# RWKV inverse: streaming only the 32 changed columns of each 64-column block

## The chip, the cores and the metric

The kernel runs on one core of one Trainium2 chip. The metric is device time in microseconds (us) from the start to the end of one execution; the median of three runs stands for it. Engines are named as in the profile: PE is TensorE (matmul), PEld is TensorE's weight load, DVE VectorE, ACT ScalarE, POOL GpSimd, SP SyncE, which only issues transfers.

## The reference

A two-layer backbone on 512 latent and 256 context tokens, width 1024, all in fp32. Layer 0 is grouped-query attention with an MLP, layer 1 a bidirectional RWKV-7 time mixing with an MLP. The part that matters here is the RWKV scan, per direction and head, with a 64x64 state S:

```
sa = S a_t
S  = S * w_t + sa b_t^T + v_t k_t^T
y  = S r_t
```

The kernel computes it in 12 chunks of 64 tokens. Inside a chunk the terms `sa` depend on each other through a unit triangular 64x64 matrix L, and the kernel needs the inverse of I + L (with the sign folded in) for each chunk and head. The reference has no such inverse; it is a consequence of the chunked form.

## The kernel before

Work before and after the RWKV core (attention, projections, MLPs) is big matmuls, mostly at L398. The core itself (`slots`, L1210) has 16 passes q = 2g + d: eight groups g of two heads, each in two directions d. Pass q is done in three parts that overlap with the parts of other passes: `pre` (decays, keys, the triangular matrices into MT) in slot q, `inverse` in slot q + 1, `chain` (the recurrence over the 12 chunks) in slot q + 2. The strings SLOT (L1205) write the order out by hand: every engine goes through the same list of letters p, i and c, and each letter lets one of its three generators issue its next piece. So TensorE, which is in order, meets the pieces of the inverse between those of the recurrence. Waits on semaphores inside the pieces keep the data in order.

The inverse works by doubling. Level l (0 to 5) joins blocks of width w = 2^l to blocks of 2w. XI is the inverse so far, XIT its transpose. 24 matrices (12 chunks x 2 heads) are kept as three groups of four units u, each unit holding two matrices, one in each half of the 128 partitions (HALVES). Step n = 3l + i handles group i at level l:

- the *update* U = MT^T XI into PSUM bank 0 (L1495, 8 matmuls of 64x64 by 64x64). For n < 3, at level 0, the moving operand is the identity (IDN) and not XI.
- VectorE multiplies it with the level's mask (L1547). The mask holds the identity plus the entries that this level joins, which all lie in one half of the columns: those whose block number is odd for d = 0 (even for d = 1). The product is UM (for n < 3 it is XI itself). UM shares memory with AR and shows as AR in the trace.
- the *level products* for v = n from 3 on, one step later in the order: `product_xi` (L1470) forms the next XI into bank 1, `product_xit` (L1480) the next XIT into bank 2; at the last level, v >= 15, only `product_xit` is made, into both banks.
- ScalarE copies out of banks 1 and 2 only the half of the columns that the level changes (`every_other`, L1517, L1528 and L1531), and at the last level everything, into XIF (L1535).

Before the change every matmul of these three lines streams all 64 columns of its moving operand, whatever the level. The stationary operand (the weights) always has 64 columns. In the trace's names "PS<-XI,MT" the moving operand stands first and the weights second.

Two other lines serve as comparison: L2151 (128 weight columns, 2 streamed columns, in the first 60 us) and L1254 (the cumulated decays of a pass, 128 weight columns, 128 streamed columns).

Of the kernel before, what the change touches and what calls it, by code (L numbers as in the profile page):

```python
# [34 lines left out]
C = 64  # L35
# [88 lines left out]
def build(nc, a, out):  # L124

    stack = ExitStack()
    with stack:
# [28 lines left out]
        IDN, HEAD1, SWAP, SEL = CK[:, 0:128], CK[:, 128:256], CK[:, 256:384], CK[:, 384:386]  # L156
# [55 lines left out]
        def core(name, shape, dt=F32):  # L212

            t = place(name, core_at[0], shape, dt)
            core_at[0] += -(-math.prod(shape[1:]) // 64) / 4
            return t
# [19 lines left out]
        XI = core("XI", [P, 12, C])  # L236
        XIT = core("XIT", [P, 12, C])
# [9 lines left out]
        UM = [AR[b][:, 0:4, 1, :] for b in (1, 2)]  # L247
# [10 lines left out]
        def bank(b):  # L258
            return PS[:, b * 512:(b + 1) * 512]
# [929 lines left out]
        def mt_at(u):  # L1189
            m, h = divmod(u, 2)  # L1190
            return 256 * m + 128 * h if m < TC // P else 512 * (m - 1) + 256 * h

        def mt(b, u, part):


            return MT[b][:, mt_at(u) + part * C:mt_at(u) + part * C + C]
# [268 lines left out]
        def pe_inverse(e, q):  # L1465
            d, b = q % 2, q % 3

            def product_xi(v, i, cp):
                t, o = HALVES[cp], HALVES[1 - cp]
                return e.matmul(bank(1)[t, i * C:(i + 1) * C], XIT[o, 4 * (v % 3) + i, :], UM[v % 2][o, i, :], start=True,  # L1470
                                stop=True, skip_group_check=True)

            def product_xit(v, i, cp):

                o = HALVES[1 - cp]
                if v < 15:
                    out = bank(2)[o, i * C:(i + 1) * C]
                else:
                    out = bank(1 + i % 2)[HALVES[cp ^ (i % 2)], i // 2 * C:(i // 2 + 1) * C]
                return e.matmul(out, UM[v % 2][o, i, :], XIT[o, 4 * (v % 3) + i, :], start=True, stop=True,  # L1480
                                skip_group_check=True)

            for n in range(19):
                if n < 18:
                    e.wait_ge(um_ready, 18 * q + n)
                    if n < 3:
                        e.wait_ge(lta_ready, 3 * q + n + 1)
                    elif n >= 6:
                        e.wait_ge(xi_ready, 12 * q + n - 5)
                    e.nop(nofuse=True)  # L1490
                    for i in range(4):
                        for cp, t in enumerate(HALVES):
                            u = 4 * (n % 3) + i
                            o = HALVES[1 - cp] if n >= 3 else t
                            mm = e.matmul(bank(0)[o, i * C:(i + 1) * C], mt(b, u, 0)[t],  # L1495
                                          XI[t, u, :] if n >= 3 else IDN[t, t], start=True, stop=True,
                                          skip_group_check=True)
                    mm.then_inc(u_done, 1)
                yield
                if n >= 4:  # L1500
                    v = n - 1
                    e.wait_ge(um_ready, 18 * q + v + 1)
                    if v < 6:
                        e.wait_ge(xit_init, 6 * q + 2 * (v % 3) + 2)
                    e.wait_ge(xit_ready, 15 * q + v - 3)
                    if v < 15:
                        e.wait_ge(xi_ready, 12 * q + v - 3)
                    e.nop(nofuse=True)
                    for i in range(4):
                        for cp in range(2):  # L1510
                            if v < 15:
                                product_xi(v, i, cp)
                            mm = product_xit(v, i, cp)
                    mm.then_inc(inv_done, 1)
                yield
# [605 lines left out]
        def _(pe):  # L2121
# [117 lines left out]
            pe.wait_ge(evac_dve, U_OUT1 + 2)  # L2239
            pe.wait_ge(pads_ready, PADS)  # L2240
            slots(pe, pe_pre, pe_inverse, pe_chain)

            def og_split(e, k):
# [224 lines left out]
```

## Time and profile before

| what | value |
|---|---|
| median of 3 runs | 2493.08 us (2490.87 to 2499.34) |
| profiled execution, its own time | 2491.33 us |
| its span (first to last instruction) | 2489.1 us |
| PE busy | 2303.2 us (93%) |
| DVE, ACT, POOL busy | 1096.6, 916.0, 660.8 us |
| mean granted TensorE clock | 0.984 |

A page of the profile gives busy times of each engine, the span in 40 slices, the chain of work that ended last and the costliest groups of instructions. Rows of groups read "line engine operation out<-in shape xcount". A matmul shape "64*64 64x64" is 64 rows by 64 columns of weights, and a moving operand of 64 partitions by 64 columns. The granted clock is 1.00 at TensorE's full 2.4 GHz and 0.50 at 1.2 GHz; a stretch's number is the mean. Matmuls of one burst overlap, so their durations don't add; what counts is the distance from start to start.

### The profile page before, as it was taken

How to read it: one execution, taken by the hardware profiler on the slowest of the kernel's cores; microseconds unless marked ns; L12 is line 12 of the kernel's file. 1: busy time of each engine (PE TensorE's matmuls, PEld its weight loads, DVE VectorE, ACT ScalarE, POOL GpSimd, SP SyncE). 2: the span in 40 equal slices, each digit the busy share in tenths (PEclk: the TensorE clock that was granted, in tenths of full speed). 3: DMA queues.
4: the chain of work that ended last, by engine and by line, in shares of the span. 5: the costliest groups of instructions: out<-in, count | busy, mean ns of one | idle time of the engine just before them, and what ended most of it. 6: DMA issues, size and time to landing. Idle time of an engine off the chain costs nothing.

```text
span 2489.1 us, 65277 instructions
## 1 busy us (share of the span) xinstructions
PE 2303.2 (93%) x27611; PEld 1905.8 (77%) x27611; DVE 1096.6 (44%) x2418; ACT 916.0 (37%) x1627; POOL 660.8 (27%) x481
## 2 busy tenths in 40 slices
PE   5998899899999999999988888888888889999998
PEld 3776677788888888878857777777777768888887
DVE  2326666451121211463355666666666645411213
ACT  3555555352120312452224344244244223422324
POOL 0334555303322332213301111111121110344442
PEclk9999999999999999999999999999999999999999
DMA  8124556112122112123410000000000011323321
GB/s 250 52 51 153 172 171 184 39 63 69 51 68 67 54 64 68 51 77 119 136 50 23 12 15 23 12 15 23 12 15 23 4 53 52 102 85 101 101 94 59
DMA packets 172316, 176.38 MB, mean 71 GB/s; under 512 B 26512, under 2 KB 160032, under 8 KB 172064
## 3 DMA queue, kind: packets, MB, share of 16 engines
q1 hardware_dynamic: 172064, 172.62, 22.2%
q8 instruction: 207, 3.39, 0.6%
q14 instruction: 45, 0.37, 0.1%
HBM read 161.06 MB, written 11.53 MB: 69 GB/s over the span
## 4 chain that ended last, share of the span: by engine, by line
PE 83%; DVE 7%; issue 5%; ACT 4%; POOL 1%; SPq 0%; DMA 0%; ACTq 0%; DVEq 0%; PEldq 0%
PE PS L398 38%; PE PS L1495 5%; PE PS L576 4%; PE PS L418 3%; PE PS L1480 2%; PE PS L773 2%; PE PS L754 2%; PE PS L1634 2%; PE PS L1307 2%; PE PS L1470 2%; PE PS L733 2%; PE PS L1579 1%; PE PS L763 1%; PE PS L1140 1%; PE PS L1240 1%
## 5 line engine op out<-in xcount | busy, mean ns | idle before, releaser
L378 POOL TENSOR_TENSOR WL<-RAW,WH 128x1024 fp32r<-128x1024 f32 x160 | 383.5, 2418 | 953.0 <-ACT WH L359 953.0
L398 PE MATMUL PS<-AH,WH 128*128 128x256 f32 (+1 forms) x992 | 350.9, 354 | 3.3 <-DVE AL L2356 2.4
L398 PE MATMUL PS<-AH,WL 128*128 128x256 f32 (+1 forms) x992 | 351.6, 354 | 0.0
L398 PE MATMUL PS<-AL,WH 128*128 128x256 f32 (+1 forms) x992 | 349.1, 352 | 0.0
L359 ACT ACTIVATE WH<-RAW 128x1024 fp32r<-128x1024 f32 x160 | 160.1, 1049 | 272.1 <-PE PS L398 265.6
L398 PE MATMUL PS<-BH,WL 128*128 128x512 f32 (+1 forms) x672 | 239.2, 356 | 0.0
L398 PE MATMUL PS<-BH,WH 128*128 128x512 f32 (+1 forms) x672 | 238.5, 355 | 0.0
L398 PE MATMUL PS<-BL,WH 128*128 128x512 f32 (+1 forms) x672 | 237.6, 354 | 0.0
L398 PEld LDWEIGHTS PS<-AH,WH 128*128 128x128 f32 x992 | 187.7, 189 | 31.6 <-issue 2.6
L398 PEld LDWEIGHTS PS<-AL,WH 128*128 128x128 f32 x992 | 186.9, 188 | 27.2
L398 PEld LDWEIGHTS PS<-AH,WL 128*128 128x128 f32 x992 | 187.6, 189 | 25.1
L696 DVE SCALAR_TENSOR_TENSOR X<-PS,MOD,X 128x256 f32 (+3 forms) x92 | 54.8, 652 | 341.8 <-PE PS L398 341.8
L672 DVE TENSOR_TENSOR HSQ<-HRL 128x768 f32<-128x768 f32 (+1 forms) x64 | 51.8, 851 | 317.5 <-ACT HRL L660 317.5
L1480 PE MATMUL PS<-XIT,AR 64*64 64x64 f32 x3840 | 163.3, 226 | 21.9 <-issue 21.8
L1495 PE MATMUL PS<-XI,MT 64*64 64x64 f32 x3840 | 166.9, 223 | 6.3 <-issue 3.8
L1457 POOL TENSOR_TENSOR MT<-MT,CT 128x256 f32<-128x256 f32 x48 | 39.3, 818 | 501.2 <-DVE MT L1439 501.2
L875 POOL TENSOR_TENSOR PB<-PB,SMS 128x768 f32<-128x768 f32 (+1 forms) x96 | 123.9, 1301 | 123.1 <-DVE SMS L897 122.7
L1480 PEld LDWEIGHTS PS<-XIT,AR 64*64 64x64 f32 x3840 | 128.9, 134 | 34.9 <-issue 33.6
L1495 PEld LDWEIGHTS PS<-XI,MT 64*64 64x64 f32 x3840 | 138.7, 136 | 21.1 <-issue 16.0
L1470 PE MATMUL PS<-AR,XIT 64*64 64x64 f32 x3072 | 137.6, 223 | 15.6 <-issue 12.0
L1528 ACT ACTIVATE XI<-PS 128x128 f32<-128x128 f32 x192 | 53.6, 279 | 255.9 <-PE PS L1480 255.5
L660 ACT ACTIVATE HRL<-PS 128x768 f32<-128x768 f32 (+1 forms) x64 | 41.7, 705 | 273.6 <-PE PS L398 262.3
(278 smaller groups left out, 5019.5 us busy)
## 6 DMA issues: line engine op xcount, KB each, us to landing
ADW<-l_ada_w SPq DMA_DIRECT2D x40, 1024.0 KB, 5.4
RAW<-l_mlp_up SPq DMA_DIRECT2D x64, 512.0 KB, 4.5
RAW<-l_mlp_down SPq DMA_DIRECT2D x64, 512.0 KB, 4.3
RAW<-l_w_rkv SPq DMA_DIRECT2D x24, 512.0 KB, 5.0
rwkv_scratch<-STG SPq DMA_DIRECT2D x24, 384.0 KB, 3.2
ADA<-l_ada_w SPq DMA_DIRECT2D x4, 2048.0 KB, 15.6
RAW<-l_w_in SPq DMA_DIRECT2D x16, 256.0 KB, 5.5
RAW<-l_w_out SPq DMA_DIRECT2D x16, 256.0 KB, 5.2
```

The lines of the kernel that those rows point to most:

```text
L359: e.activation(WH[:, s, rows], RAW[:, s, rows], ACT.Copy).then_inc(w_high[h], 1)
L378: e.tensor_tensor(WL[:, s, rows], RAW[:, s, rows], WH[:, s, rows], ALU.subtract).then_inc(w_split[h], 1)
L398: mm = e.matmul(dst, w[:, s, k, n * P:(n + 1) * P], r[:, k, lo:hi], start=(k == 0 and i == 0), stop=(k == KT - 1 and i == 2), skip_group_c ...
L418: mm = e.matmul(dst, w[:, s, k, n * P:(n + 1) * P], r[:, k, lo:hi], start=(k == 0 and i == 0), stop=(k == KT - 1 and i == 2), skip_group_c ...
L576: mm = e.matmul(tile_ps(4 * s + 2 * n)[:, at:at + hi - lo], w[:, s, k, n * P:(n + 1) * P], r[:, k, lo:hi], start=(k == 0 and x == 0), stop ...
L672: e.tensor_tensor(HSQ[:, n, lo:], HRL[:, n, lo:], HRL[:, n, lo:], ALU.mult).then_inc(h_sq, 1)
L696: ins = e.scalar_tensor_tensor(out=x, in0=tile_ps(4 * s + 2 * n)[:, a0:a1], scalar=gate, in1=x, op0=ALU.mult, op1=ALU.add)
L875: e.tensor_tensor(p, p, SMS[:, rs:rs + 1].to_broadcast([P, span(m) * P]), ALU.mult).then_inc(p_scaled, 1)
L1470: return e.matmul(bank(1)[t, i * C:(i + 1) * C], XIT[o, 4 * (v % 3) + i, :], UM[v % 2][o, i, :], start=True, stop=True, skip_group_check=True)
L1480: return e.matmul(out, UM[v % 2][o, i, :], XIT[o, 4 * (v % 3) + i, :], start=True, stop=True, skip_group_check=True)
L1495: mm = e.matmul(bank(0)[o, i * C:(i + 1) * C], mt(b, u, 0)[t], XI[t, u, :] if n >= 3 else IDN[t, t], start=True, stop=True, skip_group_che ...
L1528: e.activation(every_other(XI[:, four, :], v // 3, q % 2), every_other(bank(1)[:, 0:256].rearrange("p (u t) -> p u t", u=4), v // 3, q % 2 ...
```

## The change

`columns(ap, level, odd)` takes from the last 64 columns the blocks of width 2^level whose number is odd (or even), 32 columns in all. The update at L1495 for n >= 3, `product_xi`, and `product_xit` for v < 15 now stream only these columns of the moving operand and write only the same columns in PSUM. The last level's `product_xit` and the first three updates keep 64 columns, as do all weights, all masks, all copies and all waits.

```diff
@@ pe_inverse
+            def columns(ap, level, odd):
+                return ap.rearrange("p (b two w) -> p b two w", two=2, w=1 << level)[:, :, odd, :]
+
             def product_xi(v, i, cp):
                 t, o = HALVES[cp], HALVES[1 - cp]
-                return e.matmul(bank(1)[t, i * C:(i + 1) * C], XIT[o, 4 * (v % 3) + i, :], UM[v % 2][o, i, :], start=True,
-                                stop=True, skip_group_check=True)
+                return e.matmul(columns(bank(1)[t, i * C:(i + 1) * C], v // 3, d), XIT[o, 4 * (v % 3) + i, :],
+                                columns(UM[v % 2][o, i, :], v // 3, d), start=True, stop=True, skip_group_check=True)
 
             def product_xit(v, i, cp):
 
                 o = HALVES[1 - cp]
+                rows = XIT[o, 4 * (v % 3) + i, :]
                 if v < 15:
-                    out = bank(2)[o, i * C:(i + 1) * C]
+                    out = columns(bank(2)[o, i * C:(i + 1) * C], v // 3, 1 - d)
+                    rows = columns(rows, v // 3, 1 - d)
                 else:
                     out = bank(1 + i % 2)[HALVES[cp ^ (i % 2)], i // 2 * C:(i // 2 + 1) * C]
-                return e.matmul(out, UM[v % 2][o, i, :], XIT[o, 4 * (v % 3) + i, :], start=True, stop=True,
-                                skip_group_check=True)
+                return e.matmul(out, UM[v % 2][o, i, :], rows, start=True, stop=True, skip_group_check=True)
 
@@ the update
-                            mm = e.matmul(bank(0)[o, i * C:(i + 1) * C], mt(b, u, 0)[t],
-                                          XI[t, u, :] if n >= 3 else IDN[t, t], start=True, stop=True,
-                                          skip_group_check=True)
+                            out, rows = bank(0)[o, i * C:(i + 1) * C], IDN[t, t]
+                            if n >= 3:
+                                out, rows = columns(out, n // 3, d), columns(XI[t, u, :], n // 3, d)
+                            mm = e.matmul(out, mt(b, u, 0)[t], rows, start=True, stop=True, skip_group_check=True)
```

## Rows read from the trace of the kernel before

**Rows 1.** The page: busy time, then the chain's shares by engine and by line
```profile
PE 2303.2 (93%) x27611; PEld 1905.8 (77%) x27611; DVE 1096.6 (44%) x2418; ACT 916.0 (37%) x1627; POOL 660.8 (27%) x481
...
PE 83%; DVE 7%; issue 5%; ACT 4%; POOL 1%; SPq 0%; DMA 0%; ACTq 0%; DVEq 0%; PEldq 0%
PE PS L398 38%; PE PS L1495 5%; PE PS L576 4%; PE PS L418 3%; PE PS L1480 2%; PE PS L773 2%; PE PS L754 2%; PE PS L1634 2%; PE PS L1307 2%; PE PS L1470 2%; PE PS L733 2%; PE PS L1579 1%; PE PS L763 1%; PE PS L1140 1%; PE PS L1240 1%
```

**Rows 2.** Windows: stretch and length, busy us per engine, PEclk, DMA share, GB/s
```profile
1282.00:2042.00 760.00, 658.33 (x17604) 547.02 (x17602) 474.34 (x1261) 278.11 (x640) 123.82 (x153) 0.98 0.06 19
```

**Rows 3.** The chain of waits from 1282 to 2042 us, by line
```profile
by line: PE PS L1495 16.6%; issue 9.5%; PE PS L1480 7.1%; PE PS L1307 6.2%; PE PS L1634 6.0%; PE PS L1470 5.8%; PE PS L1240 3.8%; PE PS L1609 3.3%; PE PS L1247 3.1%; PE PS L1254 3.1%; PE PS L1623 3.1%; PE PS L1280 2.3%; DVE MT L1439 2.2%; P
```

**Rows 4.** The lines' instructions (duration min/median/max, ns); who waited (us, times)
```profile
L1495 PEld LDWEIGHTS PS<-XI,MT x3840: 129/135/228, 1309.6 to 2038.3; 64*64 64x64 f32 x192
L1495 PE MATMUL PS<-XI,MT x3840: 212/218/366, 1309.6 to 2038.3; 64*64 64x64 f32 x192
...
L1480 PE MATMUL PS<-XIT,AR x3840: 213/218/365, 1312.6 to 2039.9; 64*64 64x64 f32 x192
...
  ACT XI L1528: 255.5, 162
...
L1470 PE MATMUL PS<-AR,XIT x3072: 212/218/339, 1312.7 to 2034.8; 64*64 64x64 f32 x192
```

**Rows 5.** Timeline, 1443 to 1452 us: a product burst and an update burst
```profile
1445.40 0.22 PE L1470 MATMUL PS<-AR,XIT 64*64 64x64 f32 x1
...
1445.75 0.22 PE L1470 MATMUL PS<-AR,XIT 64*64 64x64 f32 x1
...
1448.40 0.57 PEld L1495 LDWEIGHTS PS<-XI,MT 64*64 64x64 f32 x16
```

**Rows 6.** Timelines of L2151 and L1254; then L2151's loads (min/median/max, ns)
```profile
51.58 1.95 PE L2151 MATMUL PS<-CK,EV 128*128 128x2 f32 x16
...
51.58 1.86 PEld L2151 LDWEIGHTS PS<-CK,EV 128*128 128x128 f32 x16 [0.84 <-issue]
...
1439.50 1.60 PE L1254 MATMUL PS<-CT,SG 128*128 128x128 f32 x12
...
1439.50 1.42 PEld L1254 LDWEIGHTS PS<-CT,SG 128*128 128x128 f32 x12
...
L2151 PEld LDWEIGHTS PS<-CK,EV x32: 186/192/192, 45.9 to 53.2; 128*128 128x128 f32 x32
```

**Rows 7.** The chain from 1400 to 1500 us, masks at L1547
```profile
1400.71 0.33 DVE AR L1547
...
1494.36 0.33 DVE AR L1547
```

**Rows 8.** Windows before and in two falls of the clock; one that kept it
```profile
1353.20:1356.60 3.40, 2.04 (x48) 1.85 (x52) 1.65 (x7) 3.35 (x4) 0.00 (x0) 0.99 0.00 0
...
1523.80:1527.20 3.40, 1.45 (x54) 1.27 (x46) 1.48 (x2) 3.39 (x6) 0.61 (x1) 1.00 0.00 0
1527.40:1530.60 3.20, 3.20 (x31) 2.98 (x29) 1.24 (x4) 1.16 (x2) 2.90 (x5) 0.50 0.43 124
...
1889.10:1892.50 3.40, 1.96 (x76) 1.72 (x70) 1.47 (x4) 0.45 (x2) 0.00 (x0) 1.00 0.02 5
```

**Rows 9.** Windows, PE alone: two slots at full clock; five with a fall
```profile
1433.50:1479.60 46.10, 40.41 (x1123) 1.00 0.06 19
1812.60:1857.50 44.90, 40.61 (x1125) 1.00 0.07 20
...
1338.80:1385.60 46.80, 41.45 (x1123) 0.96 0.01 3
...
1905.60:1952.60 47.00, 42.25 (x1123) 0.96 0.06 19
sum 234.80, PE 209.86; mean PE 41.97
```

## The prediction

> **What bounds the kernel now.** I read the page first. TensorE is the engine to watch: it is busy 93% of the span and carries 83% of the chain of waits, but most of that is the projection line L398; the three lines of the change (L1495, L1480, L1470) stand lower in that list [rows 1]. They all lie in the RWKV core, from 1282 to 2042 us. There TensorE is busy 658 of 760 us, VectorE 474, ScalarE 278, at a mean granted clock of 0.98 [rows 2]. The chain of waits over the same stretch puts 16.6% on L1495, 7.1% on L1480, 5.8% on L1470 and 9.5% on "issue" [rows 3]. So the lines of the change do lie on the path. What they would be worth is then a question about one matmul: is a matmul with 64 weight columns and 64 streamed columns held by its stream, which the change halves, or by the load of its weights, which it leaves alone?
>
> **Part 1: how many instructions.** Every fp32 matmul of the code is two loads and two matmuls in the trace: L1480 has 15 products x 8 x 16 passes x 2 = 3840 [rows 4]. Narrowed are all 3840 of the form XI,MT at L1495 (the first three steps, 768 with the identity, stay wide), 12/15 of L1480, which is 3072, and all 3072 of L1470. They come in bursts: 15 x 16 = 240 at L1495 (16 instructions on two 64x64 tiles of the array, 8 per tile) and 12 x 16 = 192 of the two product lines together (32 instructions on four tiles, again 8 per tile), 432 bursts. Nothing is added: no instruction, wait, copy or transfer. The evictions by VectorE and ScalarE keep their widths.
>
> **Part 2: the pace inside a burst.** In one product burst the matmuls of L1470 start in pairs, the first of each pair from 1445.40 to 1445.75 in six steps, 58 ns each; the burst of L1495 at 1448.40 has 8 loads per tile in 0.57 us, one of them 0.135 long: (0.57 - 0.135)/7 = 62 ns [rows 4, 5]. A stream-bound or a load-bound tile would look the same here, since both have 64 columns. The trace has one place that separates them. L2151 streams two columns against 128 weight columns, L1254 streams 128 columns against 128. The loads of L2151 take 1.86 us for 16, so (1.86 - 0.19)/15 = 111 ns each; those of L1254 1.42 us for 12, so (1.42 - 0.19)/11 = 112 ns each [rows 6]. Taking 126 of 128 streamed columns away changes the pace by 1 ns. The load alone sets it. The median load lasts 135 ns with 64 weight columns and 192 with 128 [rows 4, 6], 57 less; 112 - 57 = 55 ns, or plainly half of 112, is then what a tile needs per load of 64 columns, and 58 to 62 is what the bursts show. So I cost the narrower stream inside a burst at nothing: the load that stays hides it. Bounds: nothing, or, were the stream the limit after all, half of 58 ns at 8 matmuls per burst, 0.23 us x 432 = 100 us. I take nothing, because the row that separates the two is unambiguous, though it has 128 weight columns and not 64.
>
> **Part 3: the end of a burst.** After the last load has ended, the stream still has to run. L2151's last matmul ends 1.95 - 1.86 = 0.09 us after its last load, L1254's 1.60 - 1.42 = 0.18 us [rows 6]: 0.09 us for 126 columns, so 32 columns are worth some 25 ns (0.7 to 0.8 ns per column). VectorE or ScalarE may therefore start 25 ns earlier after each of the 432 bursts: at most 10.8 us. But few of these handovers are on the path. TensorE goes on with the next piece of the written order, and only where the chain steps from L1495 to the mask at L1547 does the end count. The longest pieces of the chain between 1400 and 1500 hold five such masks (the first and the last are shown) and no eviction of L1528 [rows 7]; ScalarE does wait long for L1480, 255.5 us in 162 times, yet it has slack [rows 4]. Five per 100 us over 760 us are 38, at 25 ns: 1 us. I take -1 us; ends 0 and -10.8.
>
> Here a page of the Trainium skill speaks against the change: "TensorEngine Tiling (Array Packing)", section Instruction Overhead, says that a matmul has about 60 cycles of overhead and that one column takes as long as 60. By that rule going from 64 to 32 columns would save next to nothing even at the end of a burst, and this term would be 0 instead of -1 us. The 0.09 us by which two columns end sooner than 128 is short of a clear verdict, since it doesn't tell how the columns below 60 count.
>
> **Part 4: the moving operand's pattern.** The 32 columns come in runs of 2, 4, 8, 16 or 32 with gaps as long. No streamed operand of the trace has such gaps. If a column with a gap cost double, 32 would cost what 64 cost now, still behind the load: nothing. If it cost four times, a tile would go at 2 x 58 ns and each burst lose 8 x 58 ns = 0.46 us, 200 us in all. I take nothing; the four-fold case is a rival with a small chance.
>
> **Part 5: the clock.** With the same pace and thinner streams TensorE moves less data per microsecond. The granted clock is 1.00 over most of the core stage, but falls to half (1.2 instead of 2.4 GHz) for stretches like that at 1527.4 [rows 8]. Before such a fall TensorE had been busy 2.04 of 3.4 us at 1353.2, and 1.45 of 3.4 at 1523.8, while ScalarE was busy throughout; but at 1889.1 it was busy 1.96 of 3.4 and kept its clock [rows 8]. A fall has a price that rows give: stretches of the core loop that start two passes apart and hold the same work took 46.1 and 44.9 us at clock 1.00 (mean 45.5), and 234.8/5 = 46.96 where a fall lay in them [rows 9]: 1.46 us per fall. (A load goes from 129 to 228 ns at the low level, a matmul from 212 to 366 [rows 4].) Five of these seven stretches have a fall, two have none; there are 16 passes and so eight such stretches, and I expect those that escape today to get one, three at most: 3 x 1.46 = +4.4 us. Ends: no more falls, or up to three per pass, 48 x 1.46 = 70 us.
>
> **Sum.** The profiled execution took 2491.33 us, span 2489.1; it is 1.75 us below the median 2493.08. 2491.33 + 0 - 1 + 0 + 4.4 = 2494.7; brought to the median, **2496 us**. A measurement of this kernel tells about 0.3% (7.5 us) from no change, so this is "the same".
>
> **Rivals.**
> - A: the stream sets the pace of a 64-column tile. For it: both have 64 columns, and the 128-column rows needn't carry over. Against it: 111 and 112 ns, and that the load alone explains 55 of the 58. Price: 13.8% (5/6 of L1495) + 5.7% + 5.8% = 25% of the 760 us of the chain are these bursts, 192 us; half is 96. With TensorE that much faster, what is late next are the hops through VectorE and the "issue" time; I let them take a third, and get -60: 2433 us. Chance 0.12.
> - B, the slower side: the clock. The thin streams make the granted clock fall once more in each of the 16 passes (each slot of some 46 us has stretches in which TensorE waits on the recurrence of the state). 16 x 1.46 = 23 us gives 2516 us; at three per pass 2563. It decides from six extra falls on (9 us). For it: the engine was partly idle before both falls of the rows, and the change takes streaming out of every inverse burst. Against it: the stretch at 1889.1, as idle as that at 1353.2, kept its clock [rows 8], and with the pace unchanged no idle time is added. Chance 0.26. The Trainium skill, "TensorE: Matmul & The Clock Gate", section What's actually happening, has the same direction: "the default state is throttled, and activity releases the throttle".
> - C: no more falls, and all 432 burst ends count: 2493.08 - 10.8 = 2482 us. Chance 0.10. Against it: TensorE is in order and busy with the next piece at nearly all of them.
> - D: the gaps in the streamed columns cost four-fold: up to 2693 us, or some tens of microseconds if only the level with runs of 2 suffers. Chance 0.05.
> - My forecast, pace unchanged and at most a handful of falls: 0.47.
>
> **How the numbers follow.** Faster: all of A (0.12) and most of C: 0.19. Slower: B, D and the upper edge of my forecast (six falls where I count three, 0.07): 0.38. The same: 0.43. The range 2476 to 2530 leaves out A (0.12), the upper part of B and D: 0.2 in all. The likeliest case by itself spans 2485 to 2503.
>
> **What would show it.** Right, if the loads of the three lines keep 129/135 ns and the bursts keep their length (16 loads of L1495 in 0.54 to 0.57 us), with the matmuls themselves shorter by about 25 ns. Rival A: a burst of 32 in 0.3 us rather than 0.5, and L1495 with half its share of the chain. Rival B: the same bursts, but a mean clock of the stretch 1282 to 2042 well under 0.98, and more half-speed stretches. Rival D: matmul starts further apart at the second level than at the fifth. The forecast is wrong if the stage from 1282 to 2042 gets shorter or longer by more than some 10 us.

## The result

The changed kernel takes 2571.16 us (median of 4 runs, 2559.07 to 2576.46), the kernel before 2493.18 us. The ratio is 1.0303, 95% interval 1.0287 to 1.032: slower by about 78 us. The forecast was 2496 us and a range up to 2530. The profiled execution took 2571.83 us, its span is 2569.6 us.

Below is the page of the changed kernel: busy times, the busy share of TensorE and its granted clock in tenths over 40 slices, and the shares of the chain. L1502 is the update (L1495 before), L1473 and L1485 are the two level products (L1470 and L1480 before).

```profile
PE 2404.1 (94%) x27611; PEld 1999.7 (78%) x27611; DVE 1101.0 (43%) x2418; ACT 915.4 (36%) x1627; POOL 660.6 (26%) x481
...
PE   5998899999999999999989889898999899999998
...
PEclk9998999999999999999977898888777957999999
...
PE 85%; DVE 6%; issue 4%; ACT 3%; DMA 1%; POOL 1%; SPq 0%; ACTq 0%; DVEq 0%; PEldq 0%
PE PS L398 37%; PE PS L1502 6%; PE PS L576 4%; PE PS L418 3%; PE PS L1473 3%; PE PS L1485 2%; PE PS L1639 2%; PE PS L773 2%; PE PS L1584 2%; PE PS L1307 2%; PE PS L754 2%; PE PS L733 1%; PE PS L1614 1%; PE PS L1628 1%; PE PS L763 1%
```

The same clock row of the kernel before:

```profile
PEclk9999999999999999999999999999999999999999
```

The instruction counts are those of before, and TensorE is busy 101 us longer although it streams less; what stands out is the clock row. The windows put the loss in one place. The first fence is the changed kernel; the columns are the stretch, its length, busy us and instructions of PE, PEld, DVE, ACT, POOL, then granted clock, DMA share and GB/s.

```profile
0.00:1282.00 1282.00, 1212.12 (x7716) 1001.93 (x7717) 487.69 (x899) 485.45 (x758) 390.40 (x267) 0.99 0.32 98
1282.00:2122.00 840.00, 758.40 (x17713) 639.01 (x17713) 485.50 (x1284) 281.61 (x647) 127.52 (x154) 0.82 0.06 17
2122.00:2569.00 447.00, 433.61 (x2186) 358.74 (x2186) 127.80 (x235) 148.32 (x222) 142.70 (x60) 0.95 0.25 83
```

The same two outer stretches of the kernel before:

```profile
0.00:1282.00 1282.00, 1211.96 (x7721) 1000.68 (x7722) 489.61 (x902) 487.03 (x759) 390.19 (x267) 0.99 0.32 98
2042.00:2489.00 447.00, 432.94 (x2290) 358.11 (x2288) 132.65 (x255) 150.85 (x229) 146.81 (x62) 0.99 0.25 83
```

Up to 1282 us nothing moved. The core stage, 760 us at clock 0.98 before [rows 2], takes 840 us at 0.82 for nearly the same number of matmuls. A mean of 0.82 between the levels 1.00 and 0.50 is 2 x 0.18 x 840 = 302 us at 1.2 GHz. With 2 x 0.05 x 447 = 45 us behind it that is some 347 us, against 2 x 0.02 x 760 + 2 x 0.01 x 447 = 39 us before. So 308 us more at the low level go with 80.5 us of span, 0.26 us lost per microsecond at 1.2 GHz.

In their pace the bursts are as forecast. These are the durations (min/median/max, ns) in the changed kernel:

```profile
L1502 PEld LDWEIGHTS PS<-XI,MT x3840: 128/135/228, 1313.0 to 2092.4; 64*64 64x64 f32 x192
L1502 PE MATMUL PS<-XI,MT x3840: 187/219/314, 1313.0 to 2092.4; 64*64 64x32 f32 x192
```

The load is unchanged (129/135/228 before [rows 4]). Of the matmuls only the shortest is 25 ns shorter (187 ns against 212); the median stayed, 219 against 218 (the ends of matmuls are modelled in these profiles). Here is a piece of the timeline at full clock: an update burst, the mask that waits for it, and the first and last of six matmul starts of one tile in a product burst:

```profile
1404.91 0.55 PEld L1502 LDWEIGHTS PS<-XI,MT 64*64 64x64 f32 x16
1404.91 0.66 PE L1502 MATMUL PS<-XI,MT 64*64 64x32 f32 x16
...
1405.62 0.42 DVE L1552 TENSOR_TENSOR AR<-PS,CT 128x256 f32<-128x256 f32 x1 [0.30 <-PE PS L1502]
...
1405.85 0.22 PE L1473 MATMUL PS<-AR,XIT 64*64 64x32 f32 x1
...
1406.14 0.22 PE L1473 MATMUL PS<-AR,XIT 64*64 64x32 f32 x1
```

(1406.14 - 1405.85)/5 = 58 ns, as with 64 columns [rows 5], and 16 loads in 0.55 us against 0.57. In the kernel before, the matmuls and the mask of the update burst whose loads run from 1448.40 to 1448.97 [rows 5] are these:

```profile
1448.44 0.67 PE L1495 MATMUL PS<-XI,MT 64*64 64x64 f32 x16
...
1449.15 0.42 DVE L1547 TENSOR_TENSOR AR<-PS,CT 128x256 f32<-128x256 f32 x1
```

After the last load has ended, the last matmul ends 0.14 us later before and 0.11 us later now, and the mask starts 0.18 and 0.16 us later. So the burst does end some 25 ns sooner, because its last matmul starts sooner after its load.

Where the clock stays at 1.00 the slots are as long as before. Windows of TensorE alone in the changed kernel: first its third slot, then the six slots whose inverse belongs to direction 0 (the fourth, sixth and so on, which hold the same work):

```profile
1344.80:1397.00 52.20, 49.32 (x1123) 0.74 0.01 3
1397.00:1444.10 47.10, 40.97 (x1105) 1.00 0.06 15
1494.60:1542.20 47.60, 40.80 (x1105) 1.00 0.05 14
1590.30:1639.50 49.20, 42.34 (x1108) 0.97 0.05 14
1690.50:1742.20 51.70, 45.64 (x1106) 0.87 0.05 13
1794.90:1848.10 53.20, 48.96 (x1105) 0.78 0.05 13
1900.20:1952.20 52.00, 47.25 (x1108) 0.82 0.05 13
```

and the same fourth and sixth slots before:

```profile
1385.60:1433.50 47.90, 41.79 (x1107) 1.00 0.05 14
1479.60:1527.00 47.40, 41.30 (x1105) 1.00 0.05 14
```

94.7 us against 95.3 for the pair: at full clock the change is worth 0.3 us a slot, some 5 us over 16, within what two slots can tell. Over the six slots the length follows the granted clock, from 47.1 us at 1.00 to 53.2 us at 0.78.

What I had not reckoned with is how long the clock stays down. Windows of the changed kernel, all engines, before, in and behind one low stretch, and one at the end of the stage with the stretch behind it:

```profile
1360.20:1363.60 3.40, 2.44 (x81) 2.10 (x77) 1.70 (x7) 3.36 (x5) 0.00 (x0) 1.00 0.02 5
1363.80:1390.90 27.10, 27.10 (x568) 25.01 (x570) 16.40 (x40) 7.60 (x23) 0.72 (x1) 0.50 0.01 3
1391.20:1394.60 3.40, 2.72 (x112) 2.47 (x109) 2.30 (x8) 1.15 (x3) 0.50 (x2) 1.00 0.02 5
...
2052.90:2156.00 103.10, 100.25 (x1167) 68.67 (x1163) 30.09 (x107) 12.80 (x43) 7.29 (x6) 0.50 0.11 34
...
2156.20:2176.00 19.80, 19.79 (x108) 17.02 (x107) 14.81 (x30) 9.74 (x14) 0.00 (x0) 1.00 0.27 86
```

The low stretch at 1363.8 is 27 us long, where that at 1527.4 before was a little over 3 [rows 8], and TensorE counts as busy for all of it. Before it fell, the engine had been busy 2.44 of 3.4 us. The one at 2052.9 runs on for 103 us. Part of it holds work that the change doesn't touch. From the last matmul of the inverse to the last one of L1628 in the recurrence (L1623 before) both kernels start the same 268 matmuls, 68 of them the 256-column ones of L1584 (L1579 before). All engines, the changed kernel and then the kernel before:

```profile
2094.30:2151.20 56.90, 56.81 (x277) 30.49 (x269) 11.63 (x45) 4.11 (x9) 4.66 (x2) 0.50 0.00 1
2039.90:2072.60 32.70, 32.45 (x282) 18.72 (x272) 11.22 (x45) 4.12 (x9) 4.66 (x2) 1.00 0.01 1
```

These 24 us of the 80.5 come from the clock alone: 0.43 us per microsecond at 1.2 GHz, with TensorE busy throughout. The Trainium skill ("TensorE: Matmul & The Clock Gate", section What's actually happening) says that activity releases the throttle; the trace agrees only if activity is not what the profile calls busy, since 27.10 us of 27.10 were busy and the clock stayed low.

### The profile page after: what moved, and what is told of

Same layout as the page of the kernel before. It is cut to its first block, busy times and chain, and to the rows that moved or that the text cites. A ratio compares the mean times of both kernels' runs of the same rounds, so it can differ in the third digit from the quotient of the medians.

```text
span 2569.6 us, 65277 instructions
## 1 busy us (share of the span) xinstructions
PE 2404.1 (94%) x27611; PEld 1999.7 (78%) x27611; DVE 1101.0 (43%) x2418; ACT 915.4 (36%) x1627; POOL 660.6 (26%) x481
## 4 chain that ended last, share of the span: by engine, by line
PE 85%; DVE 6%; issue 4%; ACT 3%; DMA 1%; POOL 1%; SPq 0%; ACTq 0%; DVEq 0%; PEldq 0%
PE PS L398 37%; PE PS L1502 6%; PE PS L576 4%; PE PS L418 3%; PE PS L1473 3%; PE PS L1485 2%; PE PS L1639 2%; PE PS L773 2%; PE PS L1584 2%; PE PS L1307 2%; PE PS L754 2%; PE PS L733 1%; PE PS L1614 1%; PE PS L1628 1%; PE PS L763 1%
## 5 line engine op out<-in xcount | busy, mean ns | idle before, releaser
L1485 PE MATMUL PS<-XIT,AR 64*64 64x32 f32 (+1 forms) x3840 | 188.5, 248 | 16.9 <-issue 16.8
L1502 PE MATMUL PS<-XI,MT 64*64 64x32 f32 x3840 | 190.4, 242 | 3.5 <-issue 2.3
L1502 PEld LDWEIGHTS PS<-XI,MT 64*64 64x64 f32 x3840 | 168.4, 161 | 18.8 <-issue 13.0
L1485 PEld LDWEIGHTS PS<-XIT,AR 64*64 64x64 f32 x3840 | 159.5, 161 | 28.7 <-issue 27.8
L1473 PE MATMUL PS<-AR,XIT 64*64 64x32 f32 x3072 | 161.4, 249 | 7.0 <-issue 6.8
L1473 PEld LDWEIGHTS PS<-AR,XIT 64*64 64x64 f32 x3072 | 144.5, 169 | 15.7 <-issue 12.2
```

The lines of the kernel that those rows point to most:

```text
L1473: return e.matmul(columns(bank(1)[t, i * C:(i + 1) * C], v // 3, d), XIT[o, 4 * (v % 3) + i, :], columns(UM[v % 2][o, i, :], v // 3, d), s ...
L1485: return e.matmul(out, UM[v % 2][o, i, :], rows, start=True, stop=True, skip_group_check=True)
L1502: mm = e.matmul(out, mt(b, u, 0)[t], rows, start=True, stop=True, skip_group_check=True)
```

## The experiments

Each kernel was timed beside runs of the kernel before; ratios carry their 95% interval. Clocks are the mean of the profiled execution.

| kernel | median us | ratio | clock |
|---|---|---|---|
| e1, 64 columns in gapped order | 2491.35 | 0.9988 to 1.0011 | 0.981 |
| e2, 32 columns without gaps | 2557.33 | 1.0223 to 1.031 | 0.930 |
| e3, updates narrow only | 2496.9 | 1.001 to 1.0073 | 0.980 |
| e4, products narrow only | 2493.52 | 1.0 to 1.0027 | 0.982 |
| e5, two columns | 2646.16 | 1.0607 to 1.0646 | 0.867 |
| e7, kernel before, idle place filled | 2486.04 | 0.9976 to 0.9995 | 0.988 |
| e8, change, idle tiles filled | 2671.97 | 1.0721 to 1.0777 | 0.929 |
| e9, before, idle tiles filled | 2633.19 | 1.0563 to 1.0649 | 0.973 |
| e10, half of each burst narrow | 2491.01 | 0.9983 to 1.0007 | 0.977 |
| e11, first direction narrow only | 2500.95 | 1.0024 to 1.0049 | 0.970 |
| e12, change, idle place filled | 2561.22 | 1.0256 to 1.0305 | 0.932 |
| e13, products narrow, idle place filled | 2492.75 | 0.9994 to 1.0015 | 0.981 |

**e1: gaps without narrowness.** Is it the gapped access or the smaller number of columns?

```diff
             def columns(ap, level, odd):
-                return ap.rearrange("p (b two w) -> p b two w", two=2, w=1 << level)[:, :, odd, :]
+                return ap.rearrange("p (b two w) -> p two b w", two=2, w=1 << level)
```

> The three lines stream all 64 columns again, but in the gapped order of the change (first the changed half in its runs of 2 to 32, then the other half). Theory 1 (the clock: the matmuls stream half the columns, TensorE is granted half its clock for much of the core stage, and that is the whole loss): as many columns as before, so 2493 us within 8 and a mean granted clock of 0.98. Theory 2 (the gapped pattern itself costs, in reading the moving operand or in writing PSUM): as slow as the changed kernel or slower, 2560 to 2640 us, with matmul starts further apart within a burst than 58 ns.

Measured: 2491.35 us, ratio 0.9999. One burst of its timeline is as long as before:

```profile
1403.71 0.54 PEld L1502 LDWEIGHTS PS<-XI,MT 64*64 64x64 f32 x16
1403.71 0.68 PE L1502 MATMUL PS<-XI,MT 64*64 64x64 f32 x16
```

Theory 2 falls: the pattern costs nothing.

**e2: narrowness without gaps.**

```diff
+                if q == 0:
+                    return ap
-                return ap.rearrange("p (b two w) -> p b two w", two=2, w=1 << level)[:, :, odd, :]
+                return ap[:, 32 * odd:32 * odd + 32]
...
-                                columns(UM[v % 2][o, i, :], v // 3, d), start=True, stop=True, skip_group_check=True)
+                                columns(UM[v % 2][o, i, :] if q == 0 else IDN[o, o], v // 3, d), start=True, stop=True,
+                                skip_group_check=True)
```

(and likewise for the other two lines).

> 32 columns in one run without gaps, taken from the identity in place of XI, XIT and UM from the second pass on; the inverse is therefore not computed. Same instructions, waits and weights as in the changed kernel. Theory 1: 2571 us within 12, clock 0.92 to 0.935. Theory 2: no gaps, so 2493 us within 8 or faster.

Measured: 2557.33 us. Its core stage looks like that of the changed kernel:

```profile
1282.00:2122.00 840.00, 756.57 (x17768) 631.37 (x17770) 487.33 (x1293) 281.80 (x647) 128.14 (x154) 0.83 0.06 17
```

Fewer columns make the loss, gaps or none. The median is 14 us under that of the changed kernel, just outside the expected 12, but the intervals of the two ratios overlap (1.0223 to 1.031 and 1.0287 to 1.032), so the difference itself isn't shown.

**e5: two columns.** The edit is e2's with `[:, 32 * odd:32 * odd + 2]`.

> All narrowed matmuls stream only two columns, taken from the identity, from the second pass on, so the inverse isn't computed; weights, waits and instruction counts are those of the changed kernel. Theory 1 (the clock; the weight load sets the pace of a burst): at a granted clock of 1.00 the loads of a burst start as far apart as before, 58 ns per tile, and each burst ends some 50 ns earlier than before the change, but the clock falls further than with 32 columns: 0.86 to 0.92 and 2575 to 2650 us. Theory 3 (the stream sets the pace, the gain is only hidden by the clock): bursts at full clock well shorter than the 0.54 to 0.57 us of 16 loads, and less than 2560 us.

Measured: 2646.16 us at a clock of 0.867, both within what theory 1 gave. Three fences of it: a burst at full clock, the durations at both levels of the clock together, and the stage.

```profile
1400.55 0.54 PEld L1505 LDWEIGHTS PS<-CK,MT 64*64 64x64 f32 x16
1400.55 0.63 PE L1505 MATMUL PS<-CK,MT 64*64 64x2 f32 x16
```

```profile
L1505 PE MATMUL PS<-CK,MT x4368: 161/242/366, 1301.8 to 2167.3; 64*64 64x2 f32 x164, 64*64 64x64 f32 x35
```

```profile
1282.00:2240.00 958.00, 902.12 (x17910) 766.35 (x17911) 504.88 (x1327) 291.61 (x664) 127.31 (x154) 0.66 0.05 16
```

This settles the pace for 64 weight columns: sixteen loads take 0.54 us with 2 streamed columns, and 0.54 (e1) to 0.57 us [rows 5] with 64. The last matmul ends 0.63 - 0.54 = 0.09 us after the last load, against 0.68 - 0.54 = 0.14 in e1. Theory 3, the forecast's rival A, falls. The stage is at 0.66 on the mean, and the loss of 155 us of span for 2 x (0.133 x 2644.3 - 0.016 x 2489.1) = 624 us more at the low level is 0.25 us per microsecond, nearly the rate of the changed kernel.

**e3 and e4: one part each.** e3 keeps `columns` only in the update, e4 only in the two products:

```diff
-                                out, rows = columns(out, n // 3, d), columns(XI[t, u, :], n // 3, d)
+                                rows = XI[t, u, :]
```

> Only the updates (3840 of the 9984 narrowed instructions) stream 32 columns, the level products stream 64. Theory 1: the clock falls less; in proportion to the streaming taken away 38% of the 78 us, so 2523 us, clock 0.96; if falls begin only once much is taken away, less, 2500 to 2510. Theory 2: 38% of the loss as well, but at a clock of 0.98.

> Only the level products (6144 of the 9984) stream 32 columns, the updates 64. Theory 1: 62% of the 78 us in proportion, 2541 us, clock 0.945; less if the falls begin late, 2510 to 2530. Theory 2: 2541 us at a clock of 0.98.

Measured: +0.41% and +0.13%. By the ratios the parts alone add up to 0.54%, 13 us; the two at once cost 78. Proportion was the wrong measure; the variant "if falls begin late" was nearer, and even its 2500 was too high. The ten runs of e3 spread more than those of e4 and e10, from 2490.02 us at a clock of 0.982 to 2512.96 at 0.971 and 2527.34 at 0.963: the same kernel, slower where its clock was lower.

**e10 and e11: the same half, spread or bunched.** Both take away half of the streaming that the change takes away. e10 narrows the units with `i % 2` in each burst, e11 all bursts of the passes with d = 0:

```diff
             def columns(ap, level, odd):
+                if d:
+                    return ap
                 return ap.rearrange("p (b two w) -> p b two w", two=2, w=1 << level)[:, :, odd, :]
```

> In every burst two of the four units stream 32 columns and two stream 64: half of the streaming that the change takes away, spread evenly. Theory 1a (the clock follows the streaming of each short stretch, and falls begin only below some level): like the two single parts, 2490 to 2503 us, clock 0.98. Theory 1b (the loss is proportional to what is taken away): half of 78, 2529 us, clock 0.955.

> The change in the passes of the first direction only (d = 0); those of the second stream 64 columns: the same half of the streaming as in the kernel with half of each burst, but taken from every second slot. Theory 1a: the slots with the narrow inverse lose as in the changed kernel, the others nothing: 2520 to 2535 us, clock 0.95 to 0.965, with the low stretches in every second slot. Theory 1c (only the total over the stage matters): as the kernel with half of each burst.

Measured: e10 is the same as before, 0.9995; e11 is slower, 1.0036 (1.0024 to 1.0049), but its 2500.95 us miss the expected 2520 to 2535. In e11 the long low stretches stand where the narrow inverses do, in every second slot. Windows of TensorE alone in pairs: a slot with the narrow inverse, and in the row under it the wide slot that ran just before it:

```profile
1387.30:1436.60 49.30, 43.17 (x1107) 0.93 0.05 14
1342.00:1387.30 45.30, 40.97 (x1124) 1.00 0.01 3
1577.20:1626.90 49.70, 44.29 (x1107) 0.90 0.05 14
1530.00:1577.20 47.20, 42.43 (x1127) 0.97 0.06 19
1863.50:1915.00 51.50, 47.68 (x1105) 0.80 0.05 13
1818.20:1863.50 45.30, 40.81 (x1125) 1.00 0.07 19
```

So the place of the streaming matters, not only its total (theory 1c falls), and the clock follows it from slot to slot. Why the loss stays small can be read slot by slot. The six slots with the inverse of direction 0 take 297.0 us in e11, against 287.8 before and 300.8 in the changed kernel: narrowed, they lose most of what they lose there. The seven wide ones between them take 322.6 us, against 326.0 before and 357.4 in the changed kernel, and the piece from the last slots to the end, where the last inverse is one of direction 1, loses nothing either. The changed kernel, the kernel before and e11:

```profile
2002.80:2569.60 566.80, 542.03 (x4307) 0.90 0.22 71
1952.50:2489.10 536.60, 507.41 (x4307) 0.98 0.23 75
1961.00:2496.00 535.00, 507.36 (x4305) 0.98 0.23 76
```

So 30 of the 80.5 us of the changed kernel are lost in this last piece, with its 103 us at the low level, and e11 is spared them.

**e7, e12 and e13: filling the idle place.** Before each of the falls at the pass ends TensorE waits some 2 us on ScalarE's table loads. The edit gives it work there, in a PSUM bank that is free:

```diff
             mm.then_inc(lv_done, 1)
+            if d == 1 and 3 <= q < NQ - 1:
+                for _ in range(2):
+                    e.matmul(bank(7), IDN, CT[:, 0:512], start=True, stop=True, skip_group_check=True)
```

> The kernel before, with two matmuls of the identity by 512 columns into a PSUM bank that is free there, in each second pass after L1318, where TensorE stands idle for about 2.2 us while ScalarE loads its tables; their 1.8 us should fit. Theory 1: six of the falls of the clock at this place go, 1.46 us each: 2482 to 2486 us, clock 0.99. If the falls come from something else: 2491 to 2500 us with the falls where they were.

Measured on the kernel before: 0.9986 (0.9976 to 0.9995), 3.6 us faster, the only kernel here whose interval lies below 1. Its median, 2486.04 us, is at the edge of what theory 1 gave. In its profiled execution (span 2479.7 us) the stretch that preceded a fall before [rows 8] is full:

```profile
1282.00:2042.00 760.00, 673.57 (x17692) 550.34 (x17692) 476.25 (x1275) 279.90 (x647) 130.09 (x154) 0.99 0.06 19
1523.80:1527.20 3.40, 3.37 (x44) 2.02 (x42) 1.70 (x3) 3.39 (x6) 0.87 (x1) 1.00 0.00 0
```

That execution is the fastest of its 12 runs (2481.89 us), so its 9 us of span are not the typical gain. None of the five falls of [rows 9] is left in it: the seven slots are at 1.00 and take 318.4 us against 326.0. One of the five, that behind 1353.2 [rows 8], wasn't at a filled place, so the filling doesn't explain all of it.

> The changed kernel with the two matmuls of 512 columns at the idle place after L1318 in each second pass. Theory 1: the place gets its streaming, but the rest of each slot stays thin: of the low stretches only those that begin there go or get shorter; 2545 to 2568 us, clock 0.93 to 0.945. Were the idle place the sole cause of the falls, 2485 to 2495 us.

On the changed kernel the same filling gives 2561.22 us. That is as theory 1 had it, and far from 2485 to 2495: the idle place is not the sole cause. Whether the filling helps here at all isn't shown. The median is 10 us lower, but beside their own runs of the kernel before the ratios are 1.028 and 1.0303, 6 us apart, and their intervals overlap.

> Level products of 32 columns, updates of 64, and the two matmuls at the idle place. Theory 1: the falls at the ends of the passes go, those inside the slots that the narrow products brought stay: 2484 to 2490 us. If the 25 ns by which narrow bursts end sooner count for something at full clock, up to 4 us less, 2480.

On e4 it gives 1.0004, no gain; my expectation of 2484 to 2490 was wrong. The narrow products seem to take back what the filling brings, and the 25 ns per burst are not to be seen in the time.

**e8 and e9: filling the idle tiles.** An attempt to give the streaming back beside the bursts:

```diff
+                    if n >= 3:
+                        e.wait_ge(xit_ready, 15 * q + max(0, n - 4))
                     e.nop(nofuse=True)
...
+                            if n >= 3:
+                                e.matmul(bank(2)[t, (4 + i) * C:(5 + i) * C], mt(b, u, 0)[t], IDN[t, t], start=True,
+                                         stop=True, skip_group_check=True)
```

> The changed kernel, with eight more 64-column matmuls of the identity in every update burst from the fourth on, on the two 64x64 tiles that the update leaves idle, into unused columns of PSUM bank 2, and one wait for ScalarE's eviction that goes with them. They run beside the burst. Theory 1: the streaming is back, so the clock is near 0.98 and the time near 2493 to 2505 us, in spite of 7200 more matmuls and loads (3840 of each). If the narrow matmuls lose time by themselves: 2571 us or more.

> The kernel before with the same eight matmuls and the same wait in every update burst: the control of e8, which shows what the filling itself costs. Theory 1: clock 0.99 or 1.00 in the core stage, 2485 to 2500 us, within 10 us of e8. If the filling costs by itself, e8 and e9 are both slower by as much.

Measured: 2671.97 and 2633.19 us. Both miss: the control itself loses 144 us, a good part of it because the added wait holds TensorE up for ScalarE's eviction, 54.1 us in the row below; what the rest is I didn't separate. In e9, by line, count, busy us and mean ns, idle us before it and what ended it:

```profile
L1498 PE MATMUL PS<-CK,MT 64*64 64x64 f32 x3600 | 165.1, 227 | 72.0 <-ACT XIT L1536 54.1 <-issue 15.0 <-ACT XIF L1540 2.1
```

The pair says little about restoring the clock. With the same filling the narrow version is 39 us behind and at 0.929 against 0.973, in the direction of theory 1, but the filling did not bring the clock back.

## Why the prediction was wrong

- *Part 1, counts*: right. 3840, 3072 and 3072 instructions have 32 columns.
- *Part 2, the pace*: right. Narrowing the stream leaves it alone, with 32 columns (58 ns) and with 2 (0.54 us for 16 loads). The rows at 128 weight columns did carry over.
- *Part 3, the end of a burst*: 25 ns per burst was right for the end: the last matmul ends 0.14, 0.11 and 0.09 us after the last load with 64, 32 and 2 columns. The sign that was to show it, matmuls shorter by 25 ns, did not come (median 218 and 219 ns); the last one starts sooner after its load instead. By the Trainium skill's rule ("TensorEngine Tiling (Array Packing)", section Instruction Overhead) one column takes as long as 60. The unchanged median fits it; the ends 0.11 and 0.09 us after the load do not. The term's size, 1 us, lies below anything the runs resolve.
- *Part 4, the gaps*: right, nothing (e1).
- *Part 5, the clock*: this step failed. It allowed for three more falls at most, in the stretches that had none, and costed each at the price of a short one, 1.46 us: +4.4 us in all. The stage has 302 us at the low level instead, in stretches up to 27 us within the slots and one of 103 us at its end. Two errors made it. I let only the places count that stood idle in the profile; in e12 the idle place at the pass ends is filled, and 70 of the 78 us remain. And against rival B I wrote that "with the pace unchanged no idle time is added", taking TensorE's busy time for what the clock responds to. The engine's busy time even rose, to 758 of 840 us, and to all of the low stretch at 1363.8, while the narrowed matmuls stream half. A row that I had shows it from the other side: 1.96 busy of 3.4 at full clock against 2.04 before a fall [rows 8]. I read it as reassurance; it says that busy time does not order the two.
- *Rival B* had the right sign and mechanism at a chance of 0.26, and its upper figure, 2563 us, comes near the 2571 measured, but by another sum: 48 short falls at 0.43 us per low microsecond (1.46/3.4), where the kernel has some 300 us in fewer, longer stretches at 0.26. That the upper figure came near is in part luck. The range should have included it.

Shown: that the number of streamed columns, not the gaps, makes the loss (e1, e2, e5); that the long low stretches follow the narrow bursts in place (e11); that slots at full clock lose nothing; that the parts don't add (e3, e4, e10). That the low clock takes the time is shown where the work is the same: 24 of the 80.5 us in the piece behind the last inverse, and the six slots of one kind that get longer as their clock falls. The four runs of the changed kernel go the same way, 2559.07 us at a clock of 0.936 up to 2576.46 at 0.920, and so do those of e3.

That it is the whole of the loss rests on sizes, and they don't all agree. The changed kernel, e2, e5 and e12 lose 0.25 or 0.26 us of span per additional microsecond at the low level. But e11 loses 6.9 us for some 70, which is 0.10, and e8 against e9 loses 33.5 us for 235, which is 0.14. So such a microsecond has no single price: it was 0.43 in the piece where TensorE was busy throughout, and less over whole spans. Why it is less, and why e11 comes out so low, is open; TensorE carries most of the chain, but waits on other engines in part. Against a fixed price stands one run of the kernel before, too, 2497.64 us with a recorded clock of 0.935: it is hardly slower than its neighbours at 0.984. It was not profiled, so where it was low, or whether the record is right, is open. No run restored the streaming at no cost of its own.

## What to carry to other kernels

Before narrowing a stream, look for what else a matmul of that form waits for: here, with as many weight columns as streamed ones, the load already took the time, and nothing was won. What the narrower stream took away is work that kept the clock up; in this stage of small tiles, with dips in its clock already, a "free" reduction cost 3%, and two reductions that cost 0.4% and 0.1% alone cost it together. Read the granted clock of the stage before and after, and cost low stretches by their length and place, not by their number: they cost 0.43 us per microsecond in a piece where TensorE was busy throughout, and 0.10 to 0.26 over whole spans.

## What the runs showed of the hardware

- The low level outlasts a fully busy engine: 27.10 of 27.10 us busy at 0.50 in the core, and in the row below 20.00 of 20 us at the end of the stage, where the 256-column matmuls of L1584 run between small ones; the clock returned at 2156. In the kernel before the same matmuls ran at 1.00.

```profile
2100.00:2120.00 20.00, 20.00 (x82) 10.23 (x82) 4.55 (x18) 0.00 (x0) 0.67 (x1) 0.50 0.00 1
```

- Narrowing half of the matmuls of every burst to 32 columns (e10) costs nothing that shows (0.9983 to 1.0007), narrowing all of them costs 3%, and two columns instead of 64 cost 6%.
- A matmul of 64 rows by 64 weight columns goes at 58 ns per tile with 64 and with 32 streamed columns, and sixteen loads on two tiles take 0.54 to 0.57 us with 64, 0.55 with 32 and 0.54 with 2.
- The last matmul of such a burst ends 0.14, 0.11 and 0.09 us after its last load with 64, 32 and 2 streamed columns.
- A streamed operand with gaps, runs of 2 to 32 fp32 values, costs no more than one without (ratio 0.9999, interval 0.9988 to 1.0011).
